# Stick-breaking logs in one softplus pass, suffix sums between the value projections, weight copies ahead of exponentials

## The reference

```python
# stick-breaking, per head; mask is kpos < tq
z = einsum('bhqd,bhkd->bhqk', qb, k) * scale
log_rem = where(mask, log_sigmoid(-z), 0.0)            # = -softplus(z)
suffix = cumsum(log_rem, axis=3, reverse=True) - log_rem
a = where(mask, exp(log_sigmoid(z) + suffix), 0.0)     # = exp(z - sum of softplus from k on)
out = a @ v
# nsa: three masked softmaxes per head (compressed, selected, window), weighted by gates
o = g_c * softmax(q kc) vc + g_s * softmax(q ks) vs + g_w * softmax(q kw) vw
x = x + concat([o_nsa, o_sb]) @ w_out
```

## Time and profile before

| | us |
|---|---|
| median of 3 runs (lowest to highest) | 1211.48 (1210.69 to 1212.39) |
| profiled execution, its own time | 1211.06 |
| its span in the profile | 1209.3 |
| PE busy | 1193.9 |
| DVE busy | 714.2 |
| ACT busy | 594.6 |
| PE idle in waits for the copies `nPT` (L812) | 4.0 |

### The profile page before, as it was taken

The page is one execution under the profiler, slowest core; times in us unless marked ns, Lnnn a source line. Parts: engine busy times, 40 slices in busy tenths (PEclk is TensorE's granted clock), DMA queues, the critical chain, the costliest instruction groups (busy, mean ns, idle before and its releaser), DMA issues.

```text
span 1209.3 us, 15370 instructions
## 1 busy us (share of the span) xinstructions
PE 1193.9 (99%) x6189; PEld 999.0 (83%) x6189; DVE 714.2 (59%) x966; ACT 594.6 (49%) x802; POOL 62.0 (5%) x104
## 2 busy tenths in 40 slices
PE   8999999999999999999999999999999998999998
PEld 7888888888889988888888888888997886888887
DVE  5666565544476766555447655456588857654452
ACT  6754454444355456434435544434557746544331
POOL 1100010000000000000004100000030001000000
PEclk9999999999999999999999999999999999999999
DMA  7744556545545444664443745462552242654530
GB/s 276 282 157 177 205 175 242 173 167 183 209 135 196 146 151 175 243 209 177 164 181 123 291 173 205 167 227 108 197 187 70 71 140 70 247 203 177 209 139 36
DMA packets 34688, 213.58 MB, mean 177 GB/s; under 512 B 4665, under 2 KB 6841, under 8 KB 10041
## 3 DMA queue, kind: packets, MB, share of 16 engines
q1 hardware_dynamic: 34617, 212.59, 49.0%
HBM read 211.53 MB, written 1.05 MB: 176 GB/s over the span
## 4 chain that ended last, share of the span: by engine, by line
PE 91%; ACT 4%; DVE 3%; issue 1%; DMA 1%; SPq 0%; POOL 0%; DVEq 0%; POOLq 0%; ACTq 0%
PE ps L320 28%; PE ps L322 28%; PE ps L321 28%; PE ps L326 4%; ACT x_nsb L1310 1%; DMA raw<-in_w_v 1%; PE ps L812 1%; DVE wlo L1465 1%; PE ps L645 1%; ACT whi L1027 1%; ACT junk L1051 0%; PE ps L625 0%; DVE x_nsb L1884 0%; PE ps L766 0%; ACT xThi L1048 0%
## 5 line engine op out<-in xcount | busy, mean ns | idle before, releaser
L1465 DVE TENSOR_TENSOR wlo<-raw,whi 128x2048 fp32r<-128x2048 f32 (+2 forms) x200 | 440.3, 2236 | 109.5 <-ACT whi L1027 109.0
L1027 ACT ACTIVATE whi<-raw 128x2048 fp32r<-128x2048 f32 (+2 forms) x200 | 365.1, 1871 | 44.4 <-DMA raw<-in_w_dn 13.1
L320 PE MATMUL ps<-whi,xThi 128*128 128x512 f32 (+2 forms) x960 | 373.8, 389 | 3.6 <-DVE xTlo L1489 1.9
L322 PE MATMUL ps<-whi,xTlo 128*128 128x512 f32 (+2 forms) x960 | 370.9, 386 | 0.0
L321 PE MATMUL ps<-wlo,xThi 128*128 128x512 f32 (+2 forms) x960 | 370.4, 386 | 0.0
L1142 ACT ACTIVATE f_sil<-ps,stats 128x256 f32<-128x256 f32 x88 | 41.6, 473 | 358.3 <-PE ps L322 357.6
L320 PEld LDWEIGHTS ps<-whi,xThi 128*128 128x128 f32 x960 | 180.4, 188 | 43.3 <-issue 3.3
L322 PEld LDWEIGHTS ps<-whi,xTlo 128*128 128x128 f32 x960 | 180.3, 188 | 36.5
L321 PEld LDWEIGHTS ps<-wlo,xThi 128*128 128x128 f32 x960 | 180.4, 188 | 35.1
L1588 DVE SCALAR_TENSOR_TENSOR f_hid<-ps,stats,f_sil 128x256 f32<-128x256 f32 x88 | 42.4, 482 | 256.7 <-ACT f_sil L1142 256.6
L320 PE MATMUL ps<-whi,f_hThi 128*128 128x512 f32 x352 | 144.9, 412 | 0.0
(11 more groups left out here) (296 smaller groups left out, 1238.0 us busy)
## 6 DMA issues: line engine op xcount, KB each, us to landing
raw<-in_w_gu SPq DMA_DIRECT2D x88, 1024.0 KB, 5.9
raw<-in_w_dn SPq DMA_DIRECT2D x44, 1024.0 KB, 6.9
raw<-in_w_u SPq DMA_DIRECT2D x8, 1024.0 KB, 5.4
raw<-in_w_ao SPq DMA_DIRECT2D x8, 1024.0 KB, 6.3
raw<-in_w_v SPq DMA_DIRECT2D x6, 1024.0 KB, 5.5
raw<-in_w_bv SPq DMA_DIRECT2D x4, 1024.0 KB, 6.1
raw<-in_w_bk SPq DMA_DIRECT2D x4, 1024.0 KB, 5.5
raw<-in_w_bq SPq DMA_DIRECT2D x4, 1024.0 KB, 5.7
```

The costliest lines, as they stand in the source:

```text
L320: e.matmul(ps, a[0], b[0], start=start, stop=False)
L322: return e.matmul(ps, a[1], b[0], start=False, stop=stop)
L1027: e.activation(slots[slot_of[i]][0][:, cs], raw_cols(i, cs), ACT.Copy).then_inc(*inc("whi", i, p))
L1465: e.tensor_tensor(lo[:, cs], raw_cols(i, cs), hi[:, cs].bitcast(F32), ALU.subtract).then_inc(*inc("wlo", i, p))
```

## The change

Four things are done.

1. The logs come from one ACT instruction for each f, `ACT.Softplus` from `ZM[f]` to `L[f]`. `minus_abs` and `logs` on DVE (eight instructions of 128x768) and the Exp and Ln on ACT (eight of 128x768) go; four softplus come. ACT now loads one table fewer in this stretch (before: exp, ln, exp; now: softplus, exp).
2. `stick_sums(0)` and `stick_sums(1)` move out of the loop, between the pieces of the value projections; in the loop, `stick_sums(f + 2)` stands where `stick_sums(f)` stood for f = 0 and 1, and for f = 2 the first half of the output product stands there, ahead of `nsa_turn(2, 1)`. DVE's `sums` and ACT's last exponential (now `stick_weights`) move with them.
3. On ACT both copies `turned_p(f, 0)` and `turned_p(f, 1)` now stand ahead of `exps(f + 1, 0)`.
4. On DVE the gates and the copy of `vcmp` stand later.

```diff
@@ PE
                     if j == 0:
-                        e.wait_ge(*at("tL", f))
+                        e.wait_ge(*at("softplus", f))
...
             turn_h1(1)
-            e.wait_ge(*at("kcT"))
+            nsa_scores(0, 0)
+            stick_sums(0)
             project(("sv", 1), GB[1], half_of(xT, 1), pair, kts=range(4), last=True)
-            nsa_scores(0, 0)
             compressed(1)
+            nsa_scores(0, 1)
             project(("sv", 0), GB[0], half_of(xT, 0), pair, kts=range(4, 8))
-            nsa_scores(0, 1)
+            stick_sums(1)
             project(("sv", 1), GB[1], half_of(xT, 1), pair, kts=range(4, 8), last=True)
...
-                stick_sums(f)
+                if f < 2:
+                    stick_sums(f + 2)
+                elif f == 2:
+                    wo.update({i: take() for i in (0, 2)})
+                    e.wait_ge(*at("olo", 1))
+                    early = out_steps(0, 0, range(0, 2), True, False, True)
+                    next(early)
                 nsa_turn(f, 1)
                 if f < 3:
-                    if f == 2:
-                        wo.update({i: take() for i in (0, 2)})
-                        e.wait_ge(*at("olo", 1))
-                        early = out_steps(0, 0, range(0, 2), True, False, True)
-                        next(early)
                     nsa_scores(f + 1, 1)
@@ ACT
+            e.wait_ge(*at("product", "used", 152))
+            for f in range(4):
+                e.wait_ge(*at("zm", f, 1))
+                e.activation(flat(L[f]), flat(ZM[f]), ACT.Softplus).then_inc(*inc("softplus", f))
...
-            for f in range(4):
-                e.wait_ge(*at("minus", f))
-                e.activation(flat(L[f]), flat(L[f]), ACT.Exp, scale=1.0, bias=0.0).then_inc(*inc("spexp", f))
-            for f in range(4):
-                e.wait_ge(*at("spexp", f))
-                e.activation(flat(L[f]), flat(L[f]), ACT.Ln, scale=1.0, bias=1.0).then_inc(*inc("softplus", f))
...
+            exps(0, 0)
+            stick_weights(0)
+            exps(0, 1)
+            keep_sv(0)
+            stick_weights(1)
+            keep_sv(1)
...
                 turned_p(f, 0)
+                turned_p(f, 1)
                 if f < 3:
                     exps(f + 1, 0)
-                e.wait_ge(*at("zsum", f, 1))
-                e.activation(flat(L[f]), flat(ZM[f]), ACT.Exp).then_inc(*inc("A", f))
-                turned_p(f, 1)
+                if f < 2:
+                    stick_weights(f + 2)
                 if f < 3:
                     split()
                     exps(f + 1, 1)
@@ DVE
-            minus_abs(0)
-            minus_abs(1)
...
-            minus_abs(2)
-            minus_abs(3)
...
             nsa_max(0, 0)
-            for f in range(3):
-                logs(f)
+            gates()
+            sums(0)
+            nsa_weights(0, 0)
+            compressed_values()
             nsa_max(0, 1)
-            nsa_weights(0, 0)
-            logs(3)
+            sums(1)
             nsa_weights(0, 1)
...
                 if f:
                     outs(f - 1)
-                sums(f)
+                if f < 2:
+                    sums(f + 2)
                 if f < 3:
                     nsa_weights(f + 1, 0)
                     nsa_max(f + 1, 1)
                     split()
                     nsa_weights(f + 1, 1)
```

More of the change, by code:

```diff
@@ L1321, in turned_p, with stick_weights, keep_sv @@
                 copy(d[0:30, 768:1024], PS[3][0:30, 256:512], "npt", f, j)
-            for t in range(2):
-                exps(0, t)
+            def stick_weights(f):
+                e.wait_ge(*at("zsum", f, 1))
+                e.activation(flat(L[f]), flat(ZM[f]), ACT.Exp).then_inc(*inc("A", f))
+            def keep_sv(t):
                 e.wait_ge(*at("product", "sv", t))
                 copy(SV[t][:, :], PS[GB[t]][:, :], "SV", t, scale=stat("r", "m", t))
+            exps(0, 0)
[4 more added lines that the diff above has]
+            keep_sv(1)
             for f in range(4):
@@ L1818, in stick_z @@
                     e.tensor_tensor(ZM[f][:, j, :], PS[banks[j]][:, 0:384], flat(strict), ALU.add).then_inc(*inc("zm", f, j))
[L1820 to L1825, removed]
             flat_blocks(0)
@@ L1863, in mixer, with gates, compressed_values @@
             split()
-            minus_abs(2)
-            minus_abs(3)
             h1_T(1)
[L1867 to L1875, removed]
+            def gates():
+                for t in range(2):
+                    g = G[:, t, :]
+                    e.wait_ge(*at("gexp", t))
+                    e.tensor_scalar(g, g, 1e38, 1.0, op0=ALU.min, op1=ALU.add).then_inc(*inc("gden", t))
+                    e.wait_ge(*at("gden", t))
+                    e.reciprocal(g, g).then_inc(*inc("gate", t))
+            def compressed_values():
+                e.wait_ge(*at("product", "cmp", 1))
+                e.wait_ge(*at("pool", "vcmp rows"))
+                e.tensor_copy(vcmp[0:30, :], PS[2][0:30, 256:320]).then_inc(*inc("vcmp"))
             def nsa_max(f, j):
@@ L1914, in sums @@
                     e.tensor_tensor(ZM[f][:, j, :], ZM[f][:, j, :], PS[6 + j][:, 0:384], ALU.subtract).then_inc(*inc("zsum", f, j))
-            def logs(f):
-                e.wait_ge(*at("softplus", f))
-                e.scalar_tensor_tensor(out=flat(L[f]), in0=flat(ZM[f]), scalar=0.0, in1=flat(L[f]), op0=ALU.max, op1=ALU.add).then_inc(*inc("tL", f))
             nsa_max(0, 0)
-            for f in range(3):
-                logs(f)
+            gates()
+            sums(0)
+            nsa_weights(0, 0)
+            compressed_values()
             nsa_max(0, 1)
-            nsa_weights(0, 0)
-            logs(3)
+            sums(1)
             nsa_weights(0, 1)
```

## The result

The changed kernel takes **1222.01 us** (median of 4 runs, 1221.76 to 1222.58) against 1211.32 us for the kernel before (4 runs, 1210.69 to 1212.39): ratio **1.0089**, 95% interval 1.0074 to 1.0103. Its profiled execution took 1221.76 us, with a span of 1220.0 us, 10.7 us over that of before.

A forecast was written before the change was run, and what follows sets the result against it. PE, busy 1193.9 of 1209.3 us, was taken as the bound. New waits 10.8 plus new clock loss 5.7 less 7.3 removed gave net +9.2 us on the profiled 1211.06: forecast 1220.5 us, range 1214.5 to 1224.

The forecast's parts named there:

- the likeliest case: The forecast itself: new PE waits come with the clock falling behind them; 68%, own range 1218 to 1223 us.
- Softplus, 0.8 us, hidden: ACT ahead of the loop: one softplus takes 0.8 us, ends before stick_sums(0) needs it, and costs PE nothing.
- Sums between the projections, 0 by themselves: Suffix sums moved ahead of the loop: PE's work unchanged, nothing waits on the way in, counted 0.
- The copies' waits go, -4.0, with -3.3 of clock: At nsa_mix: three waits for ACT's copies vanish, -4.0 us, and the half-clock loss behind them, -3.3 us.
- Chain of 7.5 us against 5.4, 2.1 us at each scores: From nsa_turn(f, 1) through ACT and DVE 7.5 us, PE's work 5.4: 2.1 us waits at nsa_scores(2, 0) and (3, 0).
- `olo` of group 1, 2.6 us: Pass 2, first output products: only the turn's 0.93 us covers the 3.53 us until DVE's olo, so PE waits 2.6.
- `nsa_turn(3, 1)`, 2.8 us: Pass 3: PE waits for PSUM banks freed by ACT's copy of (3, 0), 13.55 us against 10.7 of work: 2.8 us.
- `olo` of group 2, 1.2 us: Pass 3, out_steps right behind nsa_turn(3, 1): PE waits 1.2 us for DVE's split and two output parts.
- The clock, 4 x 1.64 - 0.85 = 5.7 us: PE at half clock behind the four longer new waits, 1.64 us each, less 0.85 falling into a wait: 5.7 us lost.
- longer at half clock: Rival: with four waits in some 40 us, PE stays slow twice as long each time, 5.7 us more, 1226; 8%.
- the clock holds: Rival: new waits come but the clock falls behind few or none of them, +3.5 us, 1215; 13%.

The follow-up runs named there:

- the scores': Changed kernel plus 8 unused identity products on PE ahead of each of nsa_scores(2, 0) and nsa_scores(3, 0), none elsewhere; 1218.64 us.
- `olo`'s added products: Changed kernel plus unused identity products on PE only ahead of the waits for olo, 14 for group 1 and 3 for group 2; 1220.09 us.
- the one with output parts first: Changed kernel with DVE's two output parts of group f - 1 ahead of nsa_max(f + 1, 0) in passes 1 and 2; 1220.12 us.
- the products behind the turn: Changed kernel with the first output products of pass 2 put back behind nsa_turn(2, 1); 1216.62 us.
- the filled kernel: Changed kernel plus unused identity products on PE ahead of nsa_scores(2, 0), nsa_scores(3, 0) and the waits for olo of groups 1 and 2; 1216.07 us.

## Why the prediction came out right, step by step

Sign and size were right: 1220.5 forecast, 1222.01 measured, inside the range and inside the likeliest case's own. The mechanism was right in the main: the copies' waits went, and new waits came at the scores and at `olo`, by the chain that was added up. That the number came so close is in part luck: the new waits were put at 10.8 us and measured 8.1, the clock behind them at 5.7 and measured 9.5, and the two errors nearly cancel. The sum also has a slip of 0.2 us: 0.4 added to 1220.3 is 1220.7, not 1220.5.

- *Softplus, 0.8 us, hidden.* 0.76 us each, and nothing by the run with it alone.
- *Sums between the projections, 0 by themselves.* PE has no wait ahead of the loop. That they take cover from passes 2 and 3 fits the run without the copies' change, where the two waits for `olo` appear; that run moves the output products too.
- *The copies' waits go, -4.0, with -3.3 of clock.* The waits are gone. The clock's part varies from run to run: in the trace with softplus alone, at 3.9 us of the same waits, it held at the first and fell at the second.
- *Chain of 7.5 us against 5.4, 2.1 us at each scores.* From the start of `nsa_turn(0, 1)` at 934.90 to the end of the maxima of (1, 1) at 942.22 + 0.08 = 942.30 it is 7.4 us; the waits are 1.91 and 1.91 us, at the places named. The two lines, of PE and of DVE:

```profile
934.90 0.60 PE L326 MATMUL ps<-ident,x_nsb 128*128 128x128 f32 x4
942.22 0.08 DVE L1887 DVE_READ_ACCUMULATOR2_ANT stats<- 128x1 f32 x1
```

- *`olo` of group 1, 2.6 us.* 3.46 us, and 3.53 with the clock held. **Here a step failed**, by 0.9 us: I took the 3.53 us from the turn to `olo` out of the old trace, where the maxima of (3, 0) waited for that turn. In the new order they wait for DVE itself, whose weights of (2, 1) are late by the same chain that holds up the scores. In the trace of the changed kernel DVE is at those weights until about 962.3, and the parts of `olo` end at 964.54 (964.13 + 0.41). The chain's delay had to be carried on into this term. The first maximum of (3, 0) in the trace of before, with its wait for the turn:

```profile
957.05 0.19 DVE L1884 CUSTOM_DVE_ANT_0 x_nsb<-ps,m_cmask 128x30 f32<-128x30 f32 x1 [1.28 <-PE ps L778]
```

In the trace of the changed kernel, the last of the weights, the same maximum, with no wait ahead of it, and the second output part:

```profile
961.06 1.30 DVE L1905 TENSOR_SCALAR x_nsb<-x_nsb,stats 128x30 f32<-128x30 f32 x6
962.27 0.18 DVE L1887 CUSTOM_DVE_ANT_0 x_nsb<-ps,m_cmask 128x30 f32<-128x30 f32 x1
...
964.13 0.41 DVE L1911 TENSOR_TENSOR xTlo<-ps,xThi 128x256 fp32r<-128x256 f32 x1
```

- *`nsa_turn(3, 1)`, 2.8 us.* No wait in the changed kernel; 2.67 to 2.70 us in four others (the changed kernel with all, with the scores' or with `olo`'s added products, and the one with output parts first), where PE ran less at half clock ahead of it. With the products behind the turn, where some 10 us ahead of it were slow, it did not come. The term was right at full clock, and the slow stretch took its place.
- *`olo` of group 2, 1.2 us.* 0.85 us.
- *The clock, 4 x 1.64 - 0.85 = 5.7 us.* 9.5 us. **The step that failed most** was to give every wait the same price of 1.64 us: the stretches ran into each other, 6.8 and 17 us long, against 3.3 us lost in all before. My rival "longer at half clock" had half of the truth, and missed that slow work also fills a wait, so that 9.5 us lost were worth only the 5.9 us that filling the waits won. I also expected half clock behind each of four waits; behind the second it came only 2.5 us later, and the one at `nsa_turn(3, 1)` did not come at all.

The Trainium skill, "TensorE: Matmul & The Clock Gate", section "HAM oscillation — how this bites in real kernels", by which gaps as short as the forecast's do not throttle, would have given 1215. The traces disagree: in the changed kernel the clock fell at 943.2 behind a gap of 1.91 us, and filling only the two gaps of 1.91 us took 3.4 us off (1222.01 to 1218.64). The rival "the clock holds" is what the filled kernel shows: 1216.07 where I had 1215.

Open: what decides whether the clock falls behind a given wait. It is not the wait's length alone: it held behind 1.50, 1.74 and 2.67 us in three of these kernels (behind the last of these, added products followed after the turn), and fell behind 0.77, 1.50, 1.73, 1.93 and 2.68 to 2.70 us in others. The wide spread of two kernels (1214 to 1220 and 1216 to 1221) has the same look, but was not traced run by run.

## What to carry to other kernels

When an order is changed so that one wait goes, follow what is queued behind the moved instructions once around the loop, through every engine, and carry the delay into each later term: here ACT's two copies went ahead, and PE waited for DVE two steps later. Count independent work (here the sums) as cover for the tightest wait before moving it to where PE has no wait; the two moves cost 1.3 and 2.7 us alone and 10.7 together (the second has the output products' place in it; putting only the products back took 5.4 us off the changed kernel). And on an engine that is busy 99% of the time, a wait costs its length plus what the clock does behind it: look for the smallest reorder that shortens the wait (one exponential moved behind three copies gave 2.7 us by the medians, though the waits shrank by only 0.6) rather than one that moves it.

## What was unexpected of the hardware

- Waits of 1.9 us were followed by 6.8 us, and a wait of 3.46 us between slow work by about 12.7 us, of continuous PE work at the granted clock of 0.50, though PE was busy throughout.
- In the same kernel the clock was still at 1.00 behind the second wait of 1.91 us and fell 2.5 us after its end, at about 960.3, ahead of the next wait.
- The clock fell behind a wait of 0.77 us in one kernel and held behind 2.67 us in another.
- Thirty-three products whose results nobody uses made the kernel 5.9 us faster (1222.01 to 1216.07).
